# Constant tables kept resident, a routing chain in 32-wide columns and wide one-hot tables in the expert stage

## The reference

```python
group_prob = softmax(tf @ w_group + b_group)          # 4 groups, the best one is taken
e_logits = (tf @ w_expert + b_expert)[best group]     # 8 experts in it, the two best are taken
gates = softmax(top_v) * g_p
h = silu(xb @ w1[e]) * (xb @ w3[e]);  y = h @ w2[e]   # 32 experts, 1024 -> 512 -> 1024
out[token] += gate * y                                # over both experts of a token
```

## Time and profile before

| what | value |
|---|---|
| timed runs | 5060.59, 5035.03, 5025.44 us |
| the profiled execution | 5021.53 us, of which its instructions span 5019.7 us |
| TensorE busy | 4154.1 us (83%) |
| DVE busy | 2246.2 us (45%) |
| ScalarE busy | 1199.2 us (24%) |
| GpSimd busy | 483.2 us (10%) |
| mean granted TensorE clock | 0.906 of full speed |
| DMA | 934.29 MB, 186 GB/s over the span |

### The profile page before, as it was taken

The page is one execution under the profiler, slowest core; times in us unless marked ns, Lnnn a source line. Parts: engine busy times, 40 slices in busy tenths (PEclk is TensorE's granted clock), DMA queues, the critical chain, the costliest instruction groups (busy, mean ns, idle before and its releaser), DMA issues. The chain is left out here.

```text
span 5019.7 us, 93420 instructions
## 1 busy us (share of the span) xinstructions
PE 4154.1 (83%) x39002; PEld 2423.9 (48%) x39002; DVE 2246.2 (45%) x3026; ACT 1199.2 (24%) x1975; POOL 483.2 (10%) x474
## 2 busy tenths in 40 slices
PE   5788979978889794999938989799688888488893
PEld 0343445657778552444314435366577774333341
DVE  0265536756656564111132564477466556410004
ACT  0122116752222120000001211277222221000001
POOL 0033220000000000000011333200000000000001
PEclk7899988989999896999978999899899998698996
DMA  9566641113232434998976665510322214489996
GB/s 403 185 160 179 186 127 44 29 58 124 87 99 87 148 143 170 380 404 357 397 302 200 170 200 153 125 28 19 118 66 62 62 40 176 178 352 379 378 427 243
DMA packets 252397, 934.29 MB, mean 186 GB/s; under 512 B 38044, under 2 KB 102172, under 8 KB 225400
## 3 DMA queue, kind: packets, MB, share of 16 engines
q1 hardware_dynamic: 210232, 783.05, 42.3%
q0 software_dynamic: 24240, 91.63, 6.8%
q10 hardware_dynamic: 17552, 54.03, 2.7%
HBM read 722.51 MB, written 166.82 MB: 177 GB/s over the span
## 5 line engine op out<-in xcount | busy, mean ns | idle before, releaser
L773 PE MATMUL ps<-w,hT 128*128 128x480 f32 (+1 forms) x2240 | 907.0, 565 | 29.6 <-issue 28.2
L2546 PE MATMUL ps<-w,xT 128*32 128x512 f32 (+2 forms) x3104 | 673.9, 619 | 70.6 <-DMA w<-in_e_w 62.0
L773 PEld LDWEIGHTS ps<-w,hT 128*128 128x128 f32 x2240 | 436.6, 197 | 477.1 <-issue 452.9
L2493 DVE TENSOR_TENSOR sg<-sg,ps 128x512 f32<-128x512 f32 x46 | 31.6, 688 | 982.6 <-ACT sg L2287 982.6
L2546 PEld LDWEIGHTS ps<-w,xT 128*32 128x32 f32 (+2 forms) x3104 | 239.9, 139 | 466.0 <-issue 453.3
L1085 DVE TENSOR_REDUCE nm<-ps 128x1 f32<-128x1280 f32 (+1 forms) x216 | 295.9, 1370 | 137.2 <-PE ps L1176 137.2
L2546 PE MATMUL ps<-w,hT 128*32 128x512 f32 (+2 forms) x1552 | 324.9, 594 | 3.5 <-ACT hT L2278 3.5
L1176 PE MATMUL ps<-KT,qs 32*128 32x512 f32 (+3 forms) x1200 | 281.6, 586 | 50.0 <-DMA ident<-in_k_ident 23.9
L1043 ACT ACTIVATE work<-ps,nm 128x1280 f32<-128x1280 f32 (+1 forms) x216 | 265.8, 1231 | 97.9 <-DVE nm L1085 93.5
L2037 PE MATMUL ps<-w_out,yT 128*128 128x512 f32 x576 | 256.6, 605 | 14.8 <-ACT yT L1885 14.8
L567 ACT ACTIVATE po<-ps 128x480 f32<-128x480 f32 (+1 forms) x140 | 76.9, 551 | 699.5 <-PE ps L773 699.5
(11 more groups left out here) (295 smaller groups left out, 5370.3 us busy)
## 6 DMA issues: line engine op xcount, KB each, us to landing
w<-in_e_w SPq DMA_DIRECT2D x192, 2048.0 KB, 21.1
wt<-in_w_mod SPq DMA_DIRECT2D x16, 3072.0 KB, 25.2
s_ye<-yo ACTq DMA_DIRECT2D x46, 512.0 KB, 10.6
w<-in_w_in SPq DMA_DIRECT2D x12, 1920.0 KB, 16.3
ra<-s_scan SPq DMA_DIRECT2D x160, 128.0 KB, 2.8
kb<-s_scan SPq DMA_DIRECT2D x160, 128.0 KB, 2.7
x<-s_x SPq DMA_DIRECT2D x36, 512.0 KB, 6.9
s_ye<-zero POOLq DMA_DIRECT2D x68, 256.0 KB, 3.2
```

The lines of the kernel that those rows point to most:

```text
L773: mm = pe.matmul(ps[:, c, 0:n], hT[i % 2][:, t, :], w[:, c, t, 0:n], start=(t == 0), stop=(t == DT - 1))
L2546: mm = pe.matmul(ps[lo:hi, bank, :], xs[:, t, lo:hi], w[p % 3][:, t, cols], start=(t == 0), stop=(t == nt - 1), skip_group_check=len(tiles ...
```

## The change

Four things are edited.

1. Twelve constant tables and the routers' biases live in buffers of the whole program (`TABLES`, 13 buffers with the new `e_col`, the numbers 0 to 31 as a column). GpSimd fills them in the scan phase of layer 0 with 18 DMAs, after the first pair of chunks (`top_done`), and waits for them (`k_in`) before it goes on to clear rows of `s_ye`, as it did before. The 13 DMAs at the head of each expert phase and the waits on `r_in`, `c_in` and `t_in` are gone.
2. The rank of the experts and what follows from it are worked out with one expert a partition, in 32 x 32 squares on 32 partitions, in place of 32 x 32 elements in each of 128 partitions. Two small matmuls (`e_col` with `at_pos`, `ones` with `at_rank`) bring the results back to a row: expert numbers in bank 4, room codes in bank 5.
3. The one-hot matrices are written with eight (places) or sixteen (blocks) to an instruction; `hot_done` counts groups of eight, and TensorE waits once a group.
4. SyncE's first round of the weight loop is written out ahead of the loop, which starts at 1.

`k_e_col` is a new input. The declarations of tiles and semaphores are changed to match, and `build` opens the tables around all phases. The diff, cut to its core:

```diff
+TABLES = {"ident": [P, P], "before": [P, P], "before_e": [NE, NE], "rev": [P, NG + NE], "br": [P, DEPTH, NG + NE],
+          "e_row": [P, NE], "m_row": [P, NT], "j_row": [1, OVER], "iota": [P, P], "token": [P, NT], "e_col": [NE, 1],
+          "pos_row": [NE, DEPTH, NE], "room_row": [NE, DEPTH, NE]}
...
                 pool.memset(state[:, 0], 0.0).then_inc(ones_set, 1)
                 if layer == 0:
+                    pool.wait_ge(top_done, PAIR)
+                    for name in ("ident", "before", "before_e", "token", "e_col"):
+                        pool.dma_start(net.table[name][:], ins["k_" + name]).then_inc(k_in, 16)
+                    for name in ("rev", "e_row", "m_row", "iota"):
+                        pool.dma_start(net.table[name][:], ins["k_" + name].partition_broadcast(P)).then_inc(k_in, 16)
+                    pool.dma_start(net.table["j_row"][:], ins["k_j_row"].partition_broadcast(1)).then_inc(k_in, 16)
+                    for l in range(DEPTH):
+                        br = net.table["br"][:, l]
+                        pool.dma_start(br[:, 0:NG], ins["r_b_group"][l].partition_broadcast(P)).then_inc(k_in, 16)
+                        pool.dma_start(br[:, NG:], ins["r_b_expert"][l].partition_broadcast(P)).then_inc(k_in, 16)
+                        pool.dma_start(net.table["pos_row"][:, l], ins["k_pos"][l].partition_broadcast(NE)
+                                       ).then_inc(k_in, 16)
+                        pool.dma_start(net.table["room_row"][:, l], ins["k_room"][l].partition_broadcast(NE)
+                                       ).then_inc(k_in, 16)
+                    pool.wait_ge(k_in, 16 * (10 + 4 * DEPTH))
                     pool.memset(zero[:], 0.0).then_inc(zero_set, 1)
...
-        grid = xg[0][:].rearrange("p (a b) -> p a b", b=NE)
...
-                sp.dma_start(ident[:], ins["k_ident"]).then_inc(c_in, 16)
...
-                sp.dma_start(token[:], ins["k_token"]).then_inc(t_in, 16)
...
                 load_in(0, 0)
-                with sp.Fori(0, (NE - 2) // 3) as i:
+                load_in(1, 1)
+                load_out(0, 0)
+                for s in (1, 2):
+                    load_in(1 + s, (1 + s) % 3)
+                    load_out(s, s)
+                with sp.Fori(1, (NE - 2) // 3) as i:
                     for s in range(3):
                         load_in(i * 3 + (1 + s), (1 + s) % 3)
                         load_out(i * 3 + s, s)
...
-                dve.wait_ge(r_in, 48)
-                dve.tensor_tensor(lg[:, T], net.logits[:, T], br[:].unsqueeze(1).broadcast_to([P, n, NG + NE]), ALU.add)
+                dve.tensor_tensor(lg[:, T], net.logits[:, T], br.unsqueeze(1).broadcast_to([P, n, NG + NE]), ALU.add)
...
                 dve.scalar_tensor_tensor(key[:], count[:], float(NE), e_row[:], ALU.mult, ALU.subtract)
                 dve.drain()
-                dve.tensor_tensor(grid, key[:].unsqueeze(1).broadcast_to([P, NE, NE]),
-                                  key[:].unsqueeze(2).broadcast_to([P, NE, NE]), ALU.is_gt)
-                dve.drain()
-                dve.tensor_reduce(rank[:], grid, AX.X, ALU.add)
-                dve.drain()
-
-                one = grid[0:1]
-                dve.tensor_tensor(one, rank[0:1, :].unsqueeze(1).broadcast_to([1, NE, NE]),
-                                  pos_row[:].unsqueeze(2).broadcast_to([1, NE, NE]), ALU.is_equal)
-                dve.drain()
-                dve.tensor_tensor(one, one, e_row[0:1, :].unsqueeze(1).broadcast_to([1, NE, NE]), ALU.mult)
-                dve.drain()
-                dve.tensor_reduce(blk[:, OVER + 1:], one, AX.X, ALU.add)
-                dve.drain()
-                dve.tensor_copy(net.blocks[:, OVER + 1:], blk[:, OVER + 1:])
+                small = slice(0, NE)
+                dve.tensor_tensor(square[:], key[small], ident[small, 0:NE], ALU.mult)
+                dve.drain()
+                dve.tensor_reduce(key_col[:], square[:], AX.X, ALU.add)
+                dve.drain()
+                dve.tensor_scalar(square[:], key[small], key_col[:], None, ALU.is_gt)
+                dve.drain()
+                dve.tensor_reduce(rank_col[:], square[:], AX.X, ALU.add)
+                dve.drain()
+                dve.tensor_scalar(at_pos[:], pos_row, rank_col[:], None, ALU.is_equal).then_inc(at_pos_done, 1)
+                dve.tensor_scalar(at_rank[:], e_row[small], rank_col[:], None, ALU.is_equal)
+                dve.drain()
+                dve.tensor_tensor(at_rank[:], at_rank[:], room_row, ALU.mult)
+                dve.drain()
+                dve.tensor_reduce(code_col[:], at_rank[:], AX.X, ALU.add)
+                dve.drain()
+                dve.tensor_scalar(at_rank[:], ident[small, 0:NE], code_col[:], None, ALU.mult).then_inc(code_done, 1)
+                dve.wait_ge(ids_ps, 1)
+                dve.tensor_copy(net.blocks[:, OVER + 1:], ps[0:1, 4, 0:NE])
                 dve.drain()
                 dve.sem_inc(ids_done, 1)
 
-                dve.tensor_tensor(grid, rank[:].unsqueeze(2).broadcast_to([P, NE, NE]),
-                                  e_row[:].unsqueeze(1).broadcast_to([P, NE, NE]), ALU.is_equal)
-                dve.drain()
-                dve.tensor_tensor(grid, grid, room_row[:].unsqueeze(1).broadcast_to([P, NE, NE]), ALU.mult)
-                dve.drain()
-                dve.tensor_reduce(tmp[:], grid, AX.X, ALU.add)
+                dve.wait_ge(code_ps, 1)
+                dve.tensor_copy(tmp[:], ps[:, 5, 0:NE])
                 dve.drain()
                 dve.tensor_scalar(base[:], tmp[:], 1.0 / 16, -7.5 / 16, ALU.mult, ALU.add)
...
                 dve.scalar_tensor_tensor(place_m[:, T], place_q[:, T], float(-P), rowf[:, T], ALU.mult, ALU.add)
                 dve.drain()
-                dve.wait_ge(t_in, 32)
-                for t in range(t0, NT):
-                    for j in range(2):
-                        i = 2 * (t - t0) + j
-                        dve.tensor_scalar(in_block(i), iota[:], place_m[:, t, j:j + 1], None, ALU.is_equal)
-                        dve.tensor_scalar(of_block(i), iota[:, 0:NB], place_q[:, t, j:j + 1], token[:, t:t + 1],
-                                          ALU.is_equal, ALU.mult)
+                m_all, q_all = (v[:, T].rearrange("p t j -> p (t j)") for v in (place_m, place_q))
+                for i in range(0, 2 * n, DT):
+                    m = min(DT, 2 * n - i)
+                    dst = xg[i // DT][:, 0:m * P].rearrange("p (i q) -> p i q", q=P)
+                    dve.tensor_tensor(dst, iota[:].unsqueeze(1).broadcast_to([P, m, P]),
+                                      m_all[:, i:i + m].unsqueeze(2).broadcast_to([P, m, P]), ALU.is_equal)
+                    if i % 16 == 0:
+                        m = min(16, 2 * n - i)
+                        dst = yo[i // 16][:, 0:m * 64].rearrange("p (i q) -> p i q", q=64)[:, :, 0:NB]
+                        dve.tensor_tensor(dst, iota[:, 0:NB].unsqueeze(1).broadcast_to([P, m, NB]),
+                                          q_all[:, i:i + m].unsqueeze(2).broadcast_to([P, m, NB]), ALU.is_equal)
                         dve.drain()
-                        dve.sem_inc(hot_done, 1)
+                        tok = token[:, t0 + i // 2:t0 + (i + m) // 2].unsqueeze(2).unsqueeze(3)
+                        dst = yo[i // 16][:, 0:m * 64].rearrange("p (t j q) -> p t j q", j=2, q=64)[:, :, :, 0:NB]
+                        dve.tensor_tensor(dst, dst, tok.broadcast_to([P, m // 2, 2, NB]), ALU.mult)
+                    dve.drain()
+                    dve.sem_inc(hot_done, 1)
...
-                pe.wait_ge(c_in, 128)
...
+                pe.wait_ge(at_pos_done, 1)
+                pe.matmul(ps[0:1, 4, 0:NE], e_col[:], at_pos[:], start=True, stop=True).then_inc(ids_ps, 1)
+                pe.wait_ge(code_done, 1)
+                pe.matmul(ps[:, 5, 0:NE], ones[0:NE, :], at_rank[:], start=True, stop=True).then_inc(code_ps, 1)
                 pe.wait_ge(nov_done, 1)
                 pe.transpose(ps[0:NE, 2, 0:P], nov[:], ident[:]).then_inc(novT_ps, 1)
                 pe.wait_ge(novT_done, 1)
                 pe.matmul(ps[:, 3, 0:NE], novT[:], before_e[:], start=True, stop=True).then_inc(ov_ps, 1)
 
                 for i in range(2 * n):
-                    pe.wait_ge(hot_done, i + 1)
+                    if i % DT == 0:
+                        pe.wait_ge(hot_done, i // DT + 1)
                     mm = pe.matmul(ps[:, 7, 0:NB], in_block(i), of_block(i), start=(i == 0), stop=(i == 2 * n - 1))
...
+        "k_e_col": np.arange(NE).astype(np.float32)[:, None],
```

More of the change, by code:

```diff
@@ L172, in __init__ @@
         self.out = out
+        self.table = {}
         self.x = nc.dram_tensor("s_x", [TOK, D], F32).ap()
@@ L1315, in scan_phase @@
         zero = sb("zero", [P, CW])
-        zero_set, ye_clear = sem("zero_set"), sem("ye_clear")
+        zero_set, ye_clear, k_in = sem("zero_set"), sem("ye_clear"), sem("k_in")
         pe_step = sem("pe_step")
@@ L2120, in expert_phase @@
```

(35 more changed lines are left out.)

19 lines of the change are left out of this document (4 added, 15 removed).

## The result

The changed kernel takes **4998.3 us** (median of 7 executions, 4978.1 to 5016.4) against 5040.6 us for the kernel before beside it (7 executions): a ratio of 0.9915, 95% interval [0.989, 0.9941]. That is 42 us less, by the interval 30 to 55; forecast were 30.6 us less and 5004 in all, within 1% of before. The time lies there and in the range 4984 to 5021. In a second comparison the changed kernel took 5001.0 us, 0.9916 [0.9902, 0.993]. The profiled execution of after spans 4996.5 us, that of before 5019.7.

The account below looks back on a forecast made before the run. The expert-stage heads were taken to bound the kernel until weights are late: 16.1 us (layer 0) plus 14.5 us (layer 1) is 30.6 us less, from the 5035.0 median to 5004 us. Range 4984 to 5021; within 1%: 0.84.

Parts of the forecast that it names:

- What bounds the kernel: Expert-stage heads: a microsecond cut from the chain key to gather is one of the program, until weights are late.
- Constants: Start of each head: with resident tables DVE begins with POOL, 5.4 us less in layer 0, 5.0 in layer 1.
- Rank: Head, key to first base: 11.3 us becomes 3.5 in layer 0, 10.9 becomes 3.5 in layer 1.
- Table: Head, one-hots to idx: TensorE's passes at 0.227 us become the bound; gains 2.9 us (layer 0), 2.1 (layer 1).
- Gather and weights: End of head: gather stays 11.2 us under weight traffic; weight stream starts 10.0 us earlier in layer 0, 9.3 in layer 1.
- The gap of 5.2 us in layer 1: First freed buffer asked for 14.5 us earlier, first eight weights landing 9.3 earlier; cost taken as nothing, at worst 5.2.
- Weight loop: SP's written-out first round: eight weights go out without a wait in both versions, so it saves nothing.
- GpSimd: Scan of layer 0: 18 DMAs take 9.7 us, landing 4.3 to 38.1; idle waits of 55 us cover them, cost nothing.
- The clock did not rise: Rival, table product: denser TensorE passes raise the clock; 37 us less, 4998; chance 0.18.
- The gather did not wait for the weights ahead: Rival, first gather: lands behind all eight weights, heads gaining only 5.9 and 2.4 us; 8 us less, 5027; chance 0.10.
- the third rival: Weight queue: a ninth weight goes out at once and the gather waits for all; 3 us slower, 5038; chance 0.04.
- Wrong if the scan of layer 0 ends later: Sign against the forecast: the scan of layer 0, where GpSimd's added DMAs were to cost nothing, ends later.

Follow-up runs that it names:

- the tables alone: Kernel before with only the resident constant tables and their 18 GpSimd DMAs added; 5034.7 us, ratio to before 0.9983.
- the head delayed: Changed kernel with 24 idle DVE products ahead of the gate computation in both layers; 5072.0 us, ratio to before 1.006.
- the long chain on resident tables: Changed kernel with the long rank chain of before put back; 5020.8 us, ratio to before 0.9941.
- truly nine weights: Changed kernel with the written-out weight round reordered so nine weights are asked for without a wait; 4999.8 us, ratio to before 0.9919.
- before's repeat: Kernel before, unchanged, timed and profiled once more; 5039.7 us, ratio to before 0.9987.
- the kernel with its weight round in the loop: Changed kernel with the first round of SP's weight loop put back into the loop; 5000.7 us, ratio to before 0.9904.
- the held weights: Changed kernel with SP holding weights behind the first four until the first gathered rows land, both layers; 4994.2 us, ratio to before 0.9907.
- the kernel with narrow one-hots: Changed kernel with the one-hots of before, written one pair at a time; 5005.3 us, ratio to before 0.9915.

## Why the prediction held, point by point

**What bounds the kernel.** This was right. Heads cut by 31 us gave stages shorter by 28.1 us in the first pair of profiles and 30.0 in the second; heads lengthened by 63 gave 60.6. Of the single steps, rank passed on 9.7 to 12.5 of 14.5 us, and for the one-hots nothing can be told from the scatter of the stages. Holding weights back shows the other half of the argument, "until the weights are late": in layer 1 a head 6.6 us shorter gained nothing once the weights behind the fourth were asked for later.

**Constants.** 5.4 and 5.0 us were forecast, and the tables alone shorten the heads by 5.6 and 5.2.

**Rank.** 7.8 and 7.4 us were forecast, and 7.4 and 7.4 measured from `key` to `base`. Layer 0 takes 3.8 and not 3.5 because of the 0.39 us with the cause "issue" ahead of `key_col`. That gap is there in all profiles with the short chain except the one with the head delayed (3.49 in layer 0). The prediction allowed up to 2 us a layer for fetching instructions that the wait for constants had hidden. But before has a like gap at the same place, right behind `key`, though DVE had waited 6.73 us for constants:

```profile
1931.87 1.22 DVE L2373 TENSOR_TENSOR xg<-key 128x1024 f32<-128x1024 f32 x1 [0.44 <-issue]
```

With the long chain on resident tables there is none (10.9 us in layer 0), and after has two others in layer 1 (0.42 and 0.43 us). So the wait did not hide it, and its cause is open. TensorE's first small product took 0.26 us where 0.63 was taken, and nothing hung on it; the second took 0.63.

**Table.** 2.9 and 2.1 us were forecast, and 3.3 and 2.5 measured. The term's reason was right: TensorE is the bound, with 0.22 us a pass against the 0.227 taken, at 0.50, and `idx` waits 2.94 us for it. TensorE started 3.44 us after the first one-hot, against 3.5.

**Gather and weights.** The gather took 11.4 us against 11.2, and the stream began 9.8 and 9.0 us earlier in its phase, against 10.0 and 9.3. The gap of 5.2 us in layer 1 shows where the prediction looked for it: SP's wait shrank from 43.2 to 37.0 us. It cost little, since TensorE's waits grew from 53.1 to 54.8 only. **Weight loop.** It gave nothing, as taken, and with truly nine weights neither stage is clearly longer. **GpSimd.** The 18 DMAs took 9.6 us (9.7 taken) and their landing 2.29, under the lower bound of 4.3, and the wait ahead of the next clearing covers both.

**The rivals.** The clock did not rise: 0.50 in the table product of layer 0 in every kernel here, TensorE's 40 passes in one piece or not. The Trainium skill ("TensorE: Matmul & The Clock Gate", Part 1: The HAM clock gate) has activity release the half rate; in this stretch the trace doesn't bear that out in the dense order either. The gather did not wait for the weights ahead: it was asked for at 1948.85 and landed at 1960.29, while a weight asked for at 1930.93, 18 us earlier, landed at 1966.47. And the ninth weight of the third rival, once it did go out, left the gather at 11.3 us.

**The sum.** 30.6 us were forecast; the heads gave 31.1 and the stages 28.1 and 30.0. That 5004 came within 6 us of 4998 is in part luck: the base of 5035 lay 5.5 us under before's later median of 5040.6, and the timings' gain of 42 is 12 us over the sum. The timings give 42 and 44 (39 against before's repeat), and the runs don't settle the 8 to 13 us between. The profiles don't show them: the two pairs span 23.2 and 34.9 us less, 29 in the mean, so the untouched stages took back 4.9 us in one pair and gave 4.9 in the other. What the timings show is a difference in the clock. In the timed executions whose clock is on record (50 of before, 13 of the changed kernel, 45 of the others; least squares with one level for each kernel) 0.001 of mean granted clock goes with 4.1 us. Before has 0.9015 in the mean, the changed kernel 0.9060. Taking 31 us at 0.50 out of 5043 explains 0.0025 of that; the other 0.002 are worth some 8 us, an estimate. Where they lie in those executions is not shown. That stages which the change doesn't touch differ by as much shows in the scan of layer 0 (columns as above), first of before, then of the changed kernel, then of the kernel with its weight round in the loop:

```profile
1090.00:1693.00 603.00, 515.20 (x12080) 448.16 (x12080) 347.71 (x440) 156.83 (x230) 37.28 (x71) 0.94 0.33 101
```

```profile
1092.00:1689.00 597.00, 507.16 (x12080) 440.45 (x12080) 347.64 (x440) 157.04 (x230) 46.98 (x89) 0.95 0.35 102
```

```profile
1089.00:1700.00 611.00, 520.16 (x12080) 451.69 (x12080) 348.16 (x440) 157.24 (x230) 47.02 (x89) 0.93 0.34 100
```

The same 12080 products are busy for 507 to 520 us, at 0.95 to 0.93, and the last two kernels do not differ there. Whether shorter heads raise the mean clock of the rest, or chance did, is open: the delayed head points to the first (0.8994, and 8 to 10 us more than its heads), the small moves of the held weights point to neither. "Wrong if the scan of layer 0 ends later" is left open in the same way. With the tables that scan took 596 to 611 us in eleven profiles, in step with the granted clock, and in before 601 and 603. At equal clock there is a hint of a cost: at 0.938 the scan took 2.6 us longer in the kernel with narrow one-hots than in the first profile of before. A line through the eleven points the same way for both profiles of before, by some 2 us, an estimate. So "cost nothing" is not shown to within 2 us.

## What to carry to other kernels

Where a stage begins with a chain of small dependent steps, read the chain in the timeline from the first instruction to the first one of the long stream, and ask of each step how wide it has to be: the 31 us came from loads that need not be repeated, from 32 x 32 work done on 128 x 1024, and from one-hots handed over a pair at a time. Before counting it as gained, see that the streams that feed the body start earlier too, or have slack as in layer 0; where they start later and have none, the gain comes back as waits for them, as in layer 1 with the weights held. When a timing moves by more than its stages do, compare the granted clocks, of the executions and of the untouched stages, before looking for another cause.

## What was not expected of the hardware

The first gather takes 11.4 us with eight 2 MB copies asked for ahead of it, of which three to four had landed, 11.3 with nine, and 4.3 with no weight moving (4.9 in layer 1, where the tail of the fourth weight was still under way). So copies in flight make it longer, and it does not queue behind all of them. And one unchanged program spreads over 34 us (5026 to 5059 in the 50 executions of before with a clock on record), in step with the granted clock; an unchanged scan differs by 14 us between profiles, in step with it too.
